# Four whole weight blocks in flight instead of eight, and a second home for the decay rows of a state-space scan

## The reference

```python
def ssd_chunked(xh, dt, a_head, b_in, c_in):
    a_cum = jnp.cumsum((dt * a_head).reshape(bsz, nc, SSD_CHUNK, g, r), axis=2)
    x_c = (xh * dt[..., None].astype(dtype)).reshape(bsz, nc, SSD_CHUNK, g, r, p)
    ...
    seg = a_cum[:, :, :, None] - a_cum[:, :, None]
    decay = jnp.exp(jnp.where(lower[:, :, None, None], seg, -jnp.inf)).astype(dtype)
    cb = jnp.einsum('bclgn,bcsgn->bclsg', c_c, b_c)
    y_diag = jnp.einsum('bclsg,bclsgr,bcsgrp->bclgrp', cb, decay, x_c)
    ...

def gated_group_rmsnorm(y, z, g):
    v = (y * jax.nn.silu(z)).astype(jnp.float32).reshape(bsz, s, SSD_GROUPS, d // SSD_GROUPS)
    v = v * lax.rsqrt(jnp.mean(v * v, axis=-1, keepdims=True) + EPS)
    return (v.reshape(bsz, s, d) * g.astype(jnp.float32)).astype(y.dtype)
```

## Time and profile before

| | us |
|---|---|
| median of 3 runs | 2839.94 (2833.87 to 2840.79) |
| the profiled execution, its own time | 2844.39 |
| its span, first to last instruction | 2842.7 |
| TensorE matmul busy | 2652.1 (93%) |
| VectorE busy | 1454.0 (51%) |
| ScalarE busy | 1251.4 (44%) |
| GpSimd busy | 81.7 (3%) |

### The profile page before, as it was taken

How to read it: one execution, slowest core, us unless ns; L and a number is a source line. 1 busy time by engine, 2 the same in 40 slices (tenths; PEclk the granted TensorE clock), 3 DMA queues, 4 the chain that set the end, 5 groups by cost and what they waited for, 6 DMA issues and landing times.

```text
span 2842.7 us, 52629 instructions
## 1 busy us (share of the span) xinstructions
PE 2652.1 (93%) x20918; PEld 2432.3 (86%) x20918; DVE 1454.0 (51%) x2513; ACT 1251.4 (44%) x2051; POOL 81.7 (3%) x155
## 2 busy tenths in 40 slices
PE   7998999999998799999788898899989998999998
PEld 7985899999995499999777676699849896899998
DVE  3233575653425676663467778722583444433333
ACT  3335353432425644442337777722672345333321
POOL 0000000000000000000001211100000000000000
PEclk9999999999999999999989999899999999999999
DMA  6410122223321023223224544422203222222231
GB/s 180 122 67 0 45 89 93 91 96 105 112 96 45 8 75 104 96 96 105 82 86 171 201 162 158 164 97 90 82 4 131 90 84 95 73 97 98 96 103 69
DMA packets 74019, 273.97 MB, mean 96 GB/s; under 512 B 9610, under 2 KB 9642, under 8 KB 73504
## 3 DMA queue, kind: packets, MB, share of 16 engines
q1 hardware_dynamic: 60816, 217.42, 22.5%
q0 software_dynamic: 13072, 54.69, 6.2%
HBM read 264.93 MB, written 7.14 MB: 96 GB/s over the span
## 4 chain that ended last, share of the span: by engine, by line
PE 80%; DVE 8%; ACT 5%; DMA 3%; issue 3%; ACTq 0%; DVEq 0%; POOL 0%; POOLq 0%; SPq 0%
PE acc L329 67%; PE acc L360 2%; DMA res_tmp<-scratch_rows 2%; PE ps L842 1%; DMA w_raw<-in_stream 1%; PE ps L360 1%; ACT w_hi L304 1%; PE ps L444 1%; DVE big L1993 1%; DVE res_tmp L1366 1%; DVE big L1284 1%; PE ps L831 1%; PE ps L1561 1%; PE acc L856 1%; DVE x_split L1362 0%
## 5 line engine op out<-in xcount | busy, mean ns | idle before, releaser
L329 PE MATMUL acc<-x_split,w_hi 128*128 128x256 f32 x7968 | 1256.4, 280 | 23.0 <-DVE x_split L1362 10.9
L329 PEld LDWEIGHTS acc<-x_split,w_hi 128*128 128x128 f32 x7968 | 1075.2, 191 | 28.7 <-issue 21.5
L310 DVE TENSOR_TENSOR w_lo<-w_raw,w_hi 128x1024 fp32r<-128x1024 f32 x405 | 493.2, 1222 | 616.2 <-ACT w_hi L304 616.2
L329 PE MATMUL acc<-x_split,w_lo 128*128 128x256 f32 x3984 | 787.7, 279 | 0.0
L304 ACT ACTIVATE w_hi<-w_raw 128x1024 fp32r<-128x1024 f32 x405 | 425.1, 1054 | 588.4 <-PE acc L329 537.0
L329 PE MATMUL acc<-big_r,w_hi 128*128 128x256 f32 x3816 | 603.5, 279 | 12.2 <-DVE big_r L1362 4.5
L329 PEld LDWEIGHTS acc<-x_split,w_lo 128*128 128x128 f32 x3984 | 610.1, 190 | 0.0
L329 PEld LDWEIGHTS acc<-big_r,w_hi 128*128 128x128 f32 x3816 | 517.5, 190 | 14.7 <-issue 8.5
L329 PE MATMUL acc<-big_r,w_lo 128*128 128x256 f32 x1908 | 387.1, 279 | 0.0
L329 PEld LDWEIGHTS acc<-big_r,w_lo 128*128 128x128 f32 x1908 | 296.1, 190 | 0.0
L1662 ACT ACTIVATE res_tmp<-res_tmp 128x512 f32<-128x512 f32 (+3 forms) x256 | 120.9, 551 | 43.5 <-DVE res_tmp L1687 42.5
(11 more groups left out here) (280 smaller groups left out, 2444.8 us busy)
## 6 DMA issues: line engine op xcount, KB each, us to landing
w_raw<-in_stream SPq DMA_DIRECT2D x405, 512.0 KB, 3.3
res_tmp<-scratch_rows POOLq DMA_DIRECT2D x128, 320.0 KB, 5.7
scratch_bias<-res_tmp POOLq DMA_DIRECT2D x1, 2560.0 KB, 55.8
res_tmp<-in_x SPq DMA_DIRECT2D x2, 1024.0 KB, 7.6
res_tmp<-scratch_bias POOLq DMA_DIRECT2D x8, 256.0 KB, 4.3
scratch_x<-res_tmp POOLq DMA_DIRECT2D x1, 2048.0 KB, 7.0
res_tmp<-scratch_x POOLq DMA_DIRECT2D x1, 2048.0 KB, 8.2
out<-res_tmp SPq DMA_DIRECT2D x8, 256.0 KB, 2.2
```

Source lines behind the costliest of these rows:

```text
L310: dve.tensor_tensor(w_lo[:, u.slot], w_raw[:, u.slot], w_hi[:, u.slot].bitcast(F32), ALU.subtract).then_inc(lo_done, 1)
L329: mm = pe.matmul(a[:, h], w, AR[:, x + k, h], start=(k == 0 and w is wh and x == hi and h.start == 0), stop=(k == total - 1 and w is wl), ...
```

## The change

Memory first: w_lo gets the same addresses as w_raw, so the subtraction writes its result over its input, and the freed room makes the arena 84 slots long instead of 76. With that, a raw slot is free only when TensorE has used the unit, and SyncE waits for that. Then the decay rows get two homes, by the parity of j: the eight DMAs of step f wait for the head products of step f - 2. Third, for groups 0 to 2 GpSimd squares the gated outputs (in ScalarE's place) and makes their high and low parts (in ScalarE's and VectorE's place); for group 3 all stays as it was. Fourth, the order within a step: on TensorE the head products stand ahead of the sum of squares; VectorE caps two quarters right behind the convolution and makes the second w_lo between the products with C times B; ScalarE copies the turned x after half of the exponentials.

```diff
-RES = 60
-TMP = 68
-N_SLOTS = 76
+RES = 64
+TMP = 72
+N_SLOTS = 84
...
-        w_raw = ctx.enter_context(nc.sbuf_tensor("w_raw", [P, RING, BLK * P], F32))
+        w_raw = nc.alloc_sbuf_tensor_at("w_raw", [P, RING, BLK * P], F32, offset=base + N_SLOTS * S * 4)
+        w_lo = nc.alloc_sbuf_tensor_at("w_lo", [P, RING, BLK * P], F32R, offset=base + N_SLOTS * S * 4)
         w_hi = ctx.enter_context(nc.sbuf_tensor("w_hi", [P, RING, BLK * P], F32R))
-        w_lo = ctx.enter_context(nc.sbuf_tensor("w_lo", [P, RING, BLK * P], F32R))
...
         def load_unit(sp, u, wait=True):
             if wait:
-                sp.wait_ge(lo_done, (u + (-RING)).count + 1)
+                sp.wait_ge(units_used, (u + (-RING)).count + 1)
...
-            def body(i):
+            def rows_in(g, j):
                 for c in range(CH):
                     for b in range(2):
-                        pool.wait_ge(ev("s_pv"), 8 * i + (2 * c + b + 1))
...
+                        pool.wait_ge(ev("s_pv"), 32 * g + (8 * j + 2 * c + b + 1))
...
+                        pool.dma_start(part(j % 2, b, c), src).then_inc(ev(f"s_row_in{j % 2}{c}"), 16)
+
+            def squares(g):
+                for k in range(4):
+                    pool.wait_ge(ev("s_v"), 4 * g + (k + 1))
+                    pool.tensor_tensor(A.at(VH, 4 * g + k), A.at(VL, 4 * g + k), A.at(VL, 4 * g + k),
+                                       ALU.mult).then_inc(ev("s_vsq"), 1)
+
+            def split(g, ks):
+                for k in ks:
+                    f = 4 * g + k
+                    pool.wait_ge(ev("s_vn"), f + 1)
+                    pool.tensor_copy(AR.at(VH, f), A.at(VL, f)).then_inc(ev("s_vhi"), 1)
+                    pool.wait_ge(ev("s_vhi"), f + 1)
+                    pool.tensor_tensor(AR.at(VL, f), A.at(VL, f), AR.at(VH, f).bitcast(F32),
+                                       ALU.subtract).then_inc(ev("s_vlo"), 1)
+
+            def group(g, since):
+                rows_in(g, 0)
+                if since > 1:
+                    split(g + (-2), (2, 3))
+                rows_in(g, 1)
+                if since:
+                    squares(g + (-1))
+                rows_in(g, 2)
+                rows_in(g, 3)
+                if since:
+                    split(g + (-1), (0, 1))
+            for g in range(GROUPS):
+                group(g, g)
+            split(GROUPS - 2, (2, 3))
...
                     if j == 0:
                         c_times_b(g, first)
+                    if j or not first:
+                        heads(4 * g + (j - 1), (j - 1) % 4, first)
                     if j == 1 and not first:
                         square_sum(g + (-1))
-                    if j or not first:
-                        heads(4 * g + (j - 1), (j - 1) % 4, first)
...
+                    cap(g, j, 0)
+                    cap(g, j, 1)
+                    if j or not first:
+                        out(4 * g + (j - 1), (j - 1) % 4)
                     split_lo(dve, uz + RING)
-                    split_lo(dve, uz + 1 + RING)
...
+                    cap(g, j, 2)
+                    times_cb(f, j, 0)
+                    split_lo(dve, uz + 1 + RING)
+                    cap(g, j, 3)
+                    times_cb(f, j, 1)
+                    times_cb(f, j, 2)
+                    times_cb(f, j, 3)
```

More of the change, by code:

```diff
@@ L1385, in build, with rows_buf, part @@
         onward = const[:, CONST["onward"]:CONST["onward"] + P]
[L1387 to L1392 removed]
+        def rows_buf(p, b):
+            at = ROWS + 10 * p + 5 * b
+            return A[:, at:at + 5].rearrange("p b n -> p (b n)")
+        def part(p, b, c):
+            return rows_buf(p, b)[:, BACK[c]:BACK[c] + S + P]
         cb_packed = A[:, CB:CB + 5].rearrange("p b n -> p (b n)")
@@ L1445, in bcdt_act @@
             act.activation(d, d, ACT.Ln).then_inc(ev("s_logdt"), 1)
-            rows = rows_buf(0)
+            rows = rows_buf(0, 0)
             act.wait_ge(ev("s_rows"), 8)
@@ L1631, in group @@
                     uz, tz = Units(UB["ssd"] + 2 * j, g, 8), Tiles(TB["ssd"] + 2 * j, g, 8)
-                    if j == 1 and not first:
-                        squares(g + (-1))
                     if j == 2:
@@ L1647, in group @@
                     act.activation(x, x, ACT.Silu).then_inc(ev("s_xt"), 1)
-                    if j == 3 and not first:
-                        highs(g + (-1))
-                    act.wait_ge(ev("s_xtt"), f + 1)
-                    act.activation(A[:, XTOK + j % 2], ps[:, 2], ACT.Copy).then_inc(ev("s_xtok"), 1)
                     table_of_exp_and_ln(act)
-                    if j == 1 and not first:
-                        rstd(g + (-1))
                     for c in range(CH):
+                        if c == 3 and j == 1 and not first:
+                            rstd(g + (-1))
+                        if c == 2:
+                            act.wait_ge(ev("s_xtt"), f + 1)
+                            act.activation(A[:, XTOK + j % 2], ps[:, 2], ACT.Copy).then_inc(ev("s_xtok"), 1)
                         act.wait_ge(ev("s_cap"), 4 * f + (c + 1))
                         for b in range(2):
-                            w = rows_buf(b)
+                            w = rows_buf(j % 2, b)
                             for k, at, n in ((0, FORE[c], LEN[c]), (1, BACK[c], LENB[c])):
@@ L1669, in ssd_act @@
             rstd(GROUPS - 1)
+            act.wait_ge(ev("s_vlo"), 4 * (GROUPS - 1))
             highs(GROUPS - 1)
@@ L1673, in ssd_dve, with cap @@
             dve.wait_ge(ev("s_tab"), 2)
-            dve.memset(small[:, 41:42], 0.0).then_inc(ev("s_pv"), 2 * CH)
+            dve.memset(small[:, 41:42], 0.0).then_inc(ev("s_pv"), 4 * CH)
             dve.memset(small[:, 42:43], 0.0).then_inc(ev("s_w"), 1)
-            def cap(f, head, c):
-                for b in range(2):
-                    dve.wait_ge(ev(f"s_row_in{b}{c}"), 16 * (f + 1))
-                x = A[:, ROWS:ROWS + 10].rearrange("p (b m) n -> p b (m n)", b=2)
+            def cap(g, j, c):
+                p, head = j % 2, g * 8 + 2 * j
+                dve.wait_ge(ev(f"s_row_in{p}{c}"), 64 * g + 32 * (j // 2 + 1))
+                x = A[:, ROWS + 10 * p:ROWS + 10 * p + 10].rearrange("p (b m) n -> p b (m n)", b=2)
                 x = x[:, :, (S + 2 * P) * c:(S + 2 * P) * c + 2 * P].rearrange("p b (k n) -> p b k n", k=2)
@@ L1687, in cap, with times_cb @@
                 dve.tensor_tensor(x, x, own, ALU.min).then_inc(ev("s_cap"), 1)
-            def times_cb(f, b, c):
-                dve.wait_ge(ev("s_e"), 8 * f + (2 * c + b + 1))
-                w, cb = part(b, c), cb_packed[:, BACK[c]:BACK[c] + S + P]
-                dve.tensor_tensor(w, w, cb, ALU.mult).then_inc(ev("s_w"), 1)
+            def times_cb(f, j, c):
+                for b in range(2):
+                    dve.wait_ge(ev("s_e"), 8 * f + (2 * c + b + 1))
+                    w, cb = part(j % 2, b, c), cb_packed[:, BACK[c]:BACK[c] + S + P]
+                    dve.tensor_tensor(w, w, cb, ALU.mult).then_inc(ev("s_w"), 1)
             def out(f, j):
                 v = A.at(VL, f)
-                dve.wait_ge(ev("s_pv"), 8 * f + 4 * CH)
+                dve.wait_ge(ev("s_pv"), 8 * f + 6 * CH)
                 dve.wait_ge(ev("s_xt"), f + 1)
@@ L1730, in group @@
                     uz, tz = Units(UB["ssd"] + 2 * j, g, 8), Tiles(TB["ssd"] + 2 * j, g, 8)
-                    x = A[:, XT + j % 2]
-                    conv5_dve(dve, tz + 1, f + 8, f + 8, x)
+                    conv5_dve(dve, tz + 1, f + 8, f + 8, A[:, XT + j % 2])
                     if j == 0:
                         table_diagonals(g)
+                    cap(g, j, 0)
+                    cap(g, j, 1)
+                    if j or not first:
+                        out(4 * g + (j - 1), (j - 1) % 4)
                     split_lo(dve, uz + RING)
-                    split_lo(dve, uz + 1 + RING)
                     if j == 2 and not first:
                         scaled(g + (-1))
-                    if j or not first:
-                        out(4 * g + (j - 1), (j - 1) % 4)
                     if j == 0:
@@ L1743, in group @@
                         dve.wait_ge(ev("s_cb_rest"), 4 * g + 4)
-                    if j == 3 and not first:
-                        lows(g + (-1))
-                    for c in range(CH + 1):
-                        if c < CH:
-                            cap(f, g * 8 + 2 * j, c)
-                        if c:
-                            times_cb(f, 0, c - 1)
-                            times_cb(f, 1, c - 1)
+                    cap(g, j, 2)
[5 more added lines that the diff above has]
+                    times_cb(f, j, 3)
             group(0, True)
```

20 lines of the change are left out of this document (7 added, 13 removed).

## The result

| | before | after |
|---|---|---|
| median, first 4 runs of each (us) | 2840.36 | 2952.60 (2948.19 to 2955.27) |
| ratio, 95% interval | | 1.0363 [1.0322, 1.0403] |
| profiled span (us) | 2842.7 | 2946.4 |
| matmul busy | 2652.1 | 2713.3 |
| VectorE busy | 1454.0 | 1467.6 |

A forecast was written before the change was run, and what follows sets the result against it. Bounds: TensorE in products, three engines in the scan, ScalarE's order at stage ends. Forecast: 2844.4 + 34 (stage ends) + 23 (start) - 30 (scan) + 12 (GpSimd) = 2883.4, or 2879 on the median's footing; range 2848 to 2912 us.

The forecast's parts named there:

- the inside of product stages: Inside products: late weight loads are hidden, since a unit late by 3.4 us is used four tiles later; zero.
- Start of the program: First tiles: loads of units 4 to 7 now go behind GpSimd's bias write and land late; +23 us, bounds +8 and +40.
- Stage ends: At thirteen stage ends, ScalarE's split waits for a load landing 3.4 us after TensorE's last matmul; +34 us, bounds +28 and +40.
- The three norms that overlap a product's tail: Part of the +34: where a norm overlaps a product's last tiles, the late second split delays the scale; 5.3 us together.
- The scan: Scan: two homes for decay rows and the new order shorten TensorE's path by 30 us; GpSimd's arithmetic takes 12 back.
- GpSimd's arithmetic: Scan: 36 GpSimd instructions hold VectorE 0.85 us each, partly in idle time; +12 us, bounds 0 and +31.
- The lock: Rival, scan: GpSimd's arithmetic costs VectorE 1.37 us each, +31 in all, so the scan gains nothing; 2898 us, chance 0.17.
- The start did not stall until the write's end: Rival, program start: late loads come only when the bias write is done; +40 in place of +23, 2896 us, chance 0.10.
- little of the ring's cost is real: Rival: start costs +8, half the stage ends are covered (17), scan gains its full 30; 2835 us, same as before, chance 0.07.
- faster: Rival: loads still come early enough, late-load terms near zero, only the scan's -30 stands; 2810 us, chance 0.09.
- It doesn't do what it says: Rival, scan: the second home frees nothing, as broadcasts are not late for want of room; no size or chance given.
- signs named for the scan: Groups 75 to 80 us, waits before transposes under 10, row waits nearly gone, GpSimd instructions 0.7 to 1.4 us.

The follow-up runs named there:

- b_ring: The kernel before with w_lo at the addresses of w_raw and loads that wait for used units, arena still 76 slots: 2954.1 us, ratio 1.0366.
- b_lo64: The kernel before, same waits, with w_lo placed first behind the arena, then w_raw, then w_hi; only addresses differ: 2898.3 us, ratio 1.0163.
- a_biaslate: The changed kernel with GpSimd issuing the bias write only when TensorE has used 28 units: 2964.4 us, ratio 1.0424.
- b_scanlate: The kernel before, where only the loads issued during the scan (units 216 to 247) wait for used units: 2828.7 us, ratio 0.9931.
- a_nopool: The changed kernel without arithmetic on GpSimd: squares and high parts back on ScalarE, low parts on VectorE: 2944.2 us, ratio 1.0339.
- b_wait: The kernel before with one line changed: each load waits until TensorE has used unit u - 4, w_lo keeps its memory: 2926.1 us, ratio 1.0253.
- b_both0: The kernel before without the arena's 64 spare bytes, so w_raw, w_hi and w_lo start at multiples of 128 bytes: 2931.0 us, ratio 1.0288.
- b_all64: The kernel before with the whole arena of activations 64 bytes further on and the weights where they were: 2931.8 us, ratio 1.0304.

## Why the prediction was wrong, by its steps

**The step that failed** is one that the sum didn't have. The prediction went through the memory part of the change as a matter of when a load may start, and priced the inside of product stages at zero ("hidden", bounds 0 and +6). The delays inside a product are indeed hidden: b_ring, which has late loads, runs 36.1 us behind b_lo64, which has not, when unit 42 is used, and still 36.1 us behind at unit 102. But the same edit moves w_lo from behind w_hi to ahead of it, and off its 64 bytes; that alone costs 50 us (b_lo64, 2898.3 against 2848.1). No wait shows it, and TensorE is not idle for it. The rows could have warned: the earlier trace rows has 3359 matmuls in 400 us, 118.8 ns apiece, where the window of the late product has 113.2, both at full clock and with next to no idle time. Two paces for one shape stood in the kernel before, unexplained, and I read only the busy share.

**Start of the program, +23.** Right. The first 13 units took 101.9 us against 76.0 before, and b_ring 24.9 more than b_lo64 at one pace; the splits started within 2.4 us of the times worked out from the earlier trace rows. a_biaslate takes it away.

**Stage ends, +34.** Right in mechanism, too small: outside start and scan the late loads cost 49.5 us (b_ring less b_lo64, by the events that count a unit as used; the changed kernel less b_lo64 has 46). The same events tell where. The three norms that overlap a product's tail cost 8.3, 1.5 and 7.6, together 17.4 where the sum had 5.3; all other stage ends cost 32, where it had 28.7. I had counted the second split of such a stage only; the first one now starts with its landing too, and the eight squares behind it with it:

```profile
386.08 1.06 ACT L305 ACTIVATE w_hi<-w_raw 128x1024 fp32r<-128x1024 f32 x1 [17.08 <-DMA w_raw<-in_stream]
387.04 2.54 ACT L452 ACTIVATE res_tmp<-res_tmp 128x256 f32<-128x256 f32 x8
389.79 1.06 ACT L305 ACTIVATE w_hi<-w_raw 128x1024 fp32r<-128x1024 f32 x1 [0.20 <-DMA w_raw<-in_stream]
```

TensorE waited 1.19 us for these squares at 387.5, where before it had not waited. What makes up the rest of a norm's 8 us I have not traced.

**The scan, -30 + 12 = -18.** The sum came out near (the stage took 305.7 against 325.8 before and 327.6 in b_lo64, which has the changed kernel's pace), by another way, which is luck. The gain is for the most part not the second home's or the new order's, which bring 7 on top of late loads, but that of late loads, which I had priced at nothing there. They bring 20 to 25 by themselves (b_scanlate, 325.8 to 300.8). GpSimd's arithmetic cost 7 net. Its 36 instructions lengthened VectorE's by some 22 us at the caps, products, gate and w_lo, 0.6 each against the 0.85 that I took; part of that lay in idle time.

The Trainium skill's "SBUF — State Buffer", section "Who interferes with whom", says that a VectorE instruction with two SBUF inputs and a GpSimd instruction that reads SBUF shut each other out; the trace agrees: the caps that ran beside GpSimd's arithmetic took 1.24 us on the mean and the others 0.68, and two of the gate's products 3.8 and 3.9 us, as long as three squares and their own work. VectorE's instructions with an input in PSUM were left alone: nine of the norm's twelve scalings ran beside that arithmetic and took 742 ns, like the other three. The estimate from its "GPSIMD Engine Reference", section "3.1 Elementwise", 1.1 us for a two-input instruction, holds for the shortest squares, 1.04 us, and was too low for the subtractions, 1.28 at least, and for the means, 1367 and 1569 ns. (By the prediction's own working it would take 9 us off the scan's gain, not 8.)

**The rivals.** The lock was real, but cost 7 us net where the rival had 31. The start did not stall until the write's end: three of the four loads had landed by 58, 66 and 73 us, the write only at some 82. Of "little of the ring's cost is real" and "faster" nothing was seen. "It doesn't do what it says" was wrong as well: waits for rows were 20.3 us in b_ring, with late loads and one home, and 5.0 in a_nopool, with two homes and the new order. Of the signs named for the scan, two were off: waits before the transposes fell to 14.5 us, not under 10, and GpSimd's subtractions took up to 2.1 us, not 1.4.

**The likeliest reading of the total**, with b_lo64 between the two kernels: 103.7 us of span = 54.3 pace (b_lo64 less before) + 24.8 start + 46.4 stage ends and other waits outside - 21.8 scan (the changed kernel less b_lo64). So the three terms that the prediction had, +23, +34 and -18, measured 49 together in place of 39, and the missing one was larger than their sum.

**What stays open.** Why the place matters, and what picks 113.3 or 117.8 ns at place 64: in the profiles a stretch mostly keeps its pace until TensorE pauses, and the next may have the other, but not always: in b_wait it went from 113 to 118 ns at 504.7 us in the middle of a product, behind a single interval of 148 ns. That the mix is why the kernel before spreads by 53 us and b_scanlate by 44 is argued, not shown, since only one run of each was profiled; for b_scanlate that one had 113.3 nearly throughout and was its fastest (2797.6). With it stays open how much of b_scanlate's gain of 19 us in the medians is the scan's; its rest, 24 us under that of before, speaks for most of it.

## What to carry to other kernels

When a change moves tensors in on-chip memory, its addresses are part of the change: count matmuls per microsecond in a busy stretch before and after, since a slower pace shows in no wait and no busy share. A load that is early is not free either: where another stream of transfers is on the path, holding the weights back until they are needed was worth 20 to 25 us of 326. And work handed to GpSimd is paid partly by VectorE, so it must lie beside VectorE's idle time or its reads from PSUM.

## What the runs showed of the hardware that was not expected

- Matmuls of 256 columns with weights of 128x128, a load of weights between each two, came every 113.3 to 120.0 ns on the mean, and moving weights or activations by 32 to 64 bytes was enough to change it; at one place, 64, both 113.3 and 117.8 were seen. The worst place cost 74 us (b_both0) and 84 us (b_all64) against the kernel before in the same group of runs.
- Matmuls of 512 columns in plain float32 (the products C times B) came every 429 ns in both kernels, so it is no matter of the clock.
- GpSimd's square of a 128x512 tile took 1367 ns on the mean (1.04 us at least), the subtraction 1569 (1.28) and the copy 892 (0.61), all beside a busy VectorE; two of VectorE's products of 0.69 us took 3.8 and 3.9 us while three such squares ran.
- Loads of 512 KB issued among eight broadcasts of 320 KB took 8.3 us to land (median), and 3.3 when held back until these were mostly through.
- A write of 2560 KB from 8 partitions took 54.5 to 55.8 us to land, whether or not loads ran beside it.
